# Diagonals in the transposes of the attention, and turned orders at four seams of a two-block kernel

## The reference

```python
h = rms_norm(x, g_mix) * (1 + sc1) + sh1          # sc, sh, gt from silu(c) @ w_ada + b_ada
qa, ka, va, fb, qc, kc, vc = mixer_inputs(h, w_in, ...)   # projection, head norms, rope
o = concat([global_attention(qa, ka, va, ctx...), fourier_mix(fb), window_attention(qc, kc, vc, ctx..., sink)])
x = x + gt1 * (o @ w_out)
x = x + gt2 * swiglu(rms_norm(x, g_ffn) * (1 + sc2) + sh2, w_gate, w_up, w_down)
```

```python
proj = rmsnorm(x, norm_g) @ w_in                   # 8388 columns: three attentions, their gates, merge gates
ya, yb, yc = block-sparse, top-64 and dilated attention, each * silu(its gate)
merged = g0 * (ya @ w_br_a) + g1 * (yb @ w_br_b) + g2 * (yc @ w_br_c)
x = x + merged @ w_out
```

## Time and profile before

| | us |
|---|---|
| median of 3 runs | 1604.14 (1603.93 to 1605.23) |
| profiled execution, device time | 1607.49 |
| its span | 1605.5 |
| PE busy in the span | 1538.0 |
| DVE busy | 935.6 |
| ACT busy | 672.3 |
| POOL busy | 327.1 |

### The profile page before, as it was taken

How to read it: one execution, slowest core, us unless ns; L and a number is a source line. 1 busy time by engine, 2 the same in 40 slices (tenths; PEclk the granted TensorE clock), 3 DMA queues, 4 the chain that set the end, 5 groups by cost and what they waited for, 6 DMA issues and landing times.

```text
span 1605.5 us, 23813 instructions
## 1 busy us (share of the span) xinstructions
PE 1538.0 (96%) x9443; PEld 1268.4 (79%) x9443; DVE 935.6 (58%) x1315; ACT 672.3 (42%) x1051; POOL 327.1 (20%) x267
## 2 busy tenths in 40 slices
PE   5999899999999999999999999899999999999997
PEld 3765458988888888875789998789988878898886
DVE  2745436345434456855466667788634667874356
ACT  3445444311212212535443333654454546455553
POOL 1226521100000000416200000421145211203431
PEclk9999999999999999999999999999999999999999
DMA  8437742233233232338645554645423445462342
GB/s 326 160 105 252 270 109 79 79 105 98 85 105 95 88 106 79 106 125 311 168 133 187 184 184 151 201 154 177 152 86 119 155 152 180 150 189 86 117 138 88
DMA packets 168992, 234.22 MB, mean 146 GB/s; under 512 B 8977, under 2 KB 116537, under 8 KB 168769
## 3 DMA queue, kind: packets, MB, share of 16 engines
q1 hardware_dynamic: 168896, 232.90, 45.0%
HBM read 231.83 MB, written 1.05 MB: 145 GB/s over the span
## 4 chain that ended last, share of the span: by engine, by line
PE 85%; DVE 7%; ACT 3%; DMA 2%; POOL 2%; issue 1%; SPq 0%; POOLq 0%; DVEq 0%; ACTq 0%
PE psum L713 23%; PE psum L715 23%; PE psum L714 23%; PE psum L988 3%; PE psum L1021 3%; PE psum L1008 2%; PE psum L728 2%; DVE wl L1689 2%; DMA raw<-in_w_ada 2%; PE psum L993 1%; ACT wh L1289 1%; PE psum L916 1%; DVE smax L1976 1%; PE psum L848 1%; POOL work L2412 1%
## 5 line engine op out<-in xcount | busy, mean ns | idle before, releaser
L1689 DVE TENSOR_TENSOR wl<-raw,wh 128x2048 fp32r<-128x2048 f32 (+1 forms) x170 | 388.0, 2282 | 255.8 <-ACT wh L1583 150.1
L713 PE MATMUL psum<-hTh,wh 128*128 128x256 f32 (+1 forms) x1376 | 429.0, 312 | 10.4 <-DVE hTl L1797 3.8
L714 PE MATMUL psum<-hTl,wh 128*128 128x256 f32 (+1 forms) x1376 | 424.5, 308 | 0.0
L715 PE MATMUL psum<-hTh,wl 128*128 128x256 f32 (+1 forms) x1376 | 424.3, 308 | 0.0
L713 PEld LDWEIGHTS psum<-hTh,wh 128*128 128x128 f32 x1376 | 263.6, 192 | 27.4 <-issue 7.0
L714 PEld LDWEIGHTS psum<-hTl,wh 128*128 128x128 f32 x1376 | 263.7, 192 | 12.9
L715 PEld LDWEIGHTS psum<-hTh,wl 128*128 128x128 f32 x1376 | 263.8, 192 | 12.5
L1583 ACT ACTIVATE wh<-raw 128x2048 fp32r<-128x2048 f32 x62 | 118.9, 1917 | 364.5 <-PE psum L715 364.5
L1289 ACT ACTIVATE wh<-raw 128x2048 fp32r<-128x2048 f32 (+2 forms) x108 | 202.4, 1874 | 117.2 <-PE psum L715 111.5
L713 PE MATMUL psum<-wh,hTh 128*128 128x512 f32 (+3 forms) x576 | 221.9, 385 | 14.7 <-DVE hTl L1797 6.1
L2412 POOL TENSOR_SCALAR work<-work,share 128x256 f32<-128x256 f32 (+4 forms) x118 | 168.0, 1435 | 297.8 <-DVE share L1992 297.7
(11 more groups left out here) (185 smaller groups left out, 1833.2 us busy)
## 6 DMA issues: line engine op xcount, KB each, us to landing
raw<-in_w_in SPq DMA_DIRECT2D x54, 1024.0 KB, 4.9
raw<-in_w_ada SPq DMA_DIRECT2D x48, 1024.0 KB, 5.9
raw<-in_w_gate SPq DMA_DIRECT2D x22, 1024.0 KB, 5.1
raw<-in_w_up SPq DMA_DIRECT2D x22, 1024.0 KB, 5.2
raw<-in_w_down SPq DMA_DIRECT2D x22, 1024.0 KB, 4.8
raw<-in_w_in SPq DMA_DIRECT2D x16, 768.0 KB, 4.4
raw<-in_w_out SPq DMA_DIRECT2D x8, 1024.0 KB, 4.9
raw<-in_w_out SPq DMA_DIRECT2D x16, 384.0 KB, 7.6
```

The source lines that it names most:

```text
L713: pe.matmul(o, left[0], right[0], start=first, stop=False)
L714: pe.matmul(o, left[0], right[1], start=False, stop=False)
L715: return pe.matmul(o, left[1], right[0], start=False, stop=last)
L1689: dve.tensor_tensor(wl[:, w % SPLIT, 0:m], raw[:, u % RING, 0:m], wh[:, w % SPLIT, 0:m].bitcast(F32), ALU.subtract).then_inc(lo_ready, 1)
```

## The change

There are two kinds of edits. In the attention GpSimd's multiplication is gone. VectorE makes from the shares two diagonal matrices of 128x128 per step (identity times share), and TensorE turns each chunk with an ordinary matmul by its half's diagonal, which turns and scales at once. The lag in att1 goes from 3 to 2. The rest are orders at the seams: wout1 waits at first for all but the last pair and the last Fourier part, and for those before its second half; wout2 goes on with the bank after the merge's last; the output weights of wout1 are loaded only when the last modulation half has been used; in proj2 of layer 0 the residual's normalisation and the masks' rounding stand behind block 1; VectorE's splits at the first step and near the last of an att2 are left for the next one; the gate halves come one slot later.

```diff
-TURN_LAG = (3, 2)
-HALF_GATES = [(1, 1) if i in (7, 8, 9, 10, 11) else (0, 1) if i == 18 else (1, 0) for i in range(19)]
+TURN_LAG = (2, 2)
+HALF_GATES = [(1, 1) if i in (8, 9, 10, 11, 12) else (0, 1) if i == 18 else (1, 0) for i in range(19)]
...
+        shares_first = [scr[:, 3, SEQ * n:SEQ * n + SEQ].rearrange("p (x q) -> p x q", x=2) for n in range(4)]
+        shares_second = [x.rearrange("p (x q) -> p x q", x=2) for x in (
+            csil[:, :, :].rearrange("p k j -> p (k j)"), qkg[:, :, :, :].rearrange("p a l d -> p (a l d)"))]
...
-            return ada_slots(l) + 2 * n_four(l), 2 * (6 * len(tiles_of(l)) + 4) - 3 * l
+            return ada_slots(l) + 2 * n_four(l), 2 * (6 * len(tiles_of(l)) + TURN_LAG[0] + 1) - 3 * l
...
+                if step == "wout1":
+                    behind_ada[len(units)] = plan_count.now(ada_half)
...
+                if u in behind_ada:
+                    sp.wait_ge(ada_half, behind_ada[u])
...
-                    pe.wait_ge(prob_ready, 2 * u["step"] + 2)
+                    pe.wait_ge(share_ready, u["step"] + 1)
+                    diagonal = u["shares"]
...
-                            mm = pe.transpose(o[:, P * x:P * x + P], u["score"][:, f:f + P], ident[:, :])
+                            mm = pe.matmul(o[:, P * x:P * x + P], u["score"][:, f:f + P], diagonal[:, f // u["w"], :],
+                                           start=True, stop=True, skip_group_check=True)
...
-            def wout(tiles, lhs, merged=False, in_last={}):
-                pj[0] = 0
+            def wout(tiles, lhs, merged=False, in_first={}, in_last={}):
+                if not merged:
+                    pj[0] = 0
...
-                    pe.wait_ge(mix_split, pairs_until("att1", l))
-                    pe.wait_ge(mixT_ready, c.now(mixT_ready))
+                    pe.wait_ge(mix_split, pairs_until("att1", l) - 3)
+                    pe.wait_ge(mixT_ready, c.now(mixT_ready) - 1)
+
+                    def last_mixed():
+                        pe.wait_ge(mix_split, pairs_until("att1", l))
+                        pe.wait_ge(mixT_ready, c.now(mixT_ready))
+
...
+                    wout(tiles_of(l), lambda n, t: mixT(n, P * t, P * t + P, False), in_first={(1, 0): last_mixed},
+                         in_last=in_last)
...
+                            if b == 1 and l == 0:
+                                rows_normed()
+                                dve.wait_ge(masks_loaded, 16)
+                                own(dve.tensor_copy(masks2r[:, :, :, :], masks2), masks_rounded)
...
-                    dve.reciprocal(share[:, s, :], total[:, s, :]).then_inc(share_ready, 1)
+                    link(dve.reciprocal(share[:, s, :], total[:, s, :]))
+                    if i >= u["shares_after"]:
+                        dve.wait_ge(turned, steps[i - u["shares_after"]]["turn1"])
+                    dve.tensor_tensor(u["shares"], ident[:, :].unsqueeze(1).broadcast_to([P, 2, P]),
+                                      share[:, s, :].unsqueeze(2).broadcast_to([P, 2, P]), ALU.mult)\
+                        .then_inc(share_ready, 1)
...
+                behind = TURN_LAG[0] + 2
...
-                        split_ahead()
+                        if i not in (0, n + 3):
+                            split_ahead()
...
-            def attention(steps):
-
-                for i, u in enumerate(steps):
-                    pool.wait_ge(share_ready, u["step"] + 1)
-                    for x in range(2):
-                        p = u["score"][:, x * u["w"]:x * u["w"] + u["w"]]
-                        pool.tensor_scalar(p, p, share[:, i % 4, x:x + 1], None, ALU.mult).then_inc(prob_ready, 1)
```

More of the change, by code:

```diff
@@ L344, in build_program @@
         share_ready = sem("share_ready")
-        prob_ready = sem("prob_ready")
         turned = sem("turned")
@@ L479, in build_program @@
                 u["score"] = held[:, 0:2 * u["w"]]
+                kept = shares_first if step == "att1" else shares_second
+                u["shares"], u["shares_after"] = kept[i % len(kept)], len(kept)
                 u["probT"] = work[:, at_t:at_t + 2 * u["w"]].rearrange("p (c q) -> p c q", q=P)
@@ L502, in build_program @@
         ffn_first = {}
+        behind_ada = {}
         def kview(w, k0, k1, c0, c1):
@@ L1086, in wout @@
                     wide((unit[0], unit[0] + 1), [(lambda n, t=t: left(n, t), 0, 512) for t in tiles], 512, evac_dve,
-                         in_front=in_last if hf else {})
+                         in_front=in_last if hf else in_first)
                     unit[0] += 2
@@ L1239, in _ @@
                         in_last = {(1, 3, 2): lambda: turn_rows("norm1b", 0, 0, by_tile=False)}
-                    wout(tiles_of(l), lambda n, t: mixT(n, P * t, P * t + P, False), in_last=in_last)
+                    wout(tiles_of(l), lambda n, t: mixT(n, P * t, P * t + P, False), in_first={(1, 0): last_mixed},
+                         in_last=in_last)
                 if step == "merge2":
@@ L1424, in lead @@
                         act.activation(hi, ps[OUT][:, 0:SEQ], ACT.Copy).then_inc(mix_lead, 1)
-                behind, lag = 4, TURN_LAG[second]
+                lag = TURN_LAG[second]
+                behind = 4 if second else lag + 1
                 for i in range(len(steps) + behind):
@@ L1851, in norm2, with rows_normed @@
                 c.next(rstd_ready, 2)
-                if l:
-                    return
+            def rows_normed():
                 for t in X:
@@ L2016, in attention @@
                         gate(i - 4)
-                    if not second and 0 <= i - 5 < n:
-                        keep_mixed(i - 5)
+                    if not second and 0 <= i - behind < n:
+                        keep_mixed(i - behind)
                     if i < n:
@@ L2073, in wout @@
             def wout(tiles, gated):
-                pj[0] = 0
+                if gated:
+                    pj[0] = 0
                 for hf in range(2):
@@ L2278, in _ @@
                     picks = index_picks()
-                    if l == 0:
-                        dve.wait_ge(masks_loaded, 16)
-                        own(dve.tensor_copy(masks2r[:, :, :, :], masks2), masks_rounded)
                     proj(SECOND_BLOCKS, jobs2, False, l)
@@ L2439, in _ @@
                     proj(SECOND_BLOCKS, jobs2, False)
-                if step in ("att1", "att2"):
-                    attention(att[step, l])
                 if step == "gates2":
```

## The result

The changed kernel takes 1635.36 us (median of four, 1634.74 to 1636.70) against 1604.68 us for the kernel before: a ratio of 1.0194, interval 1.0181 to 1.0208, so +30.7 us. The prediction was 1629.4 us (+25.3), range 1612 to 1643. The profiled execution took 1634.82 us.

What follows compares the result with a forecast made beforehand. The prediction took TensorE to set the time. Turns cost 40.3 us, less 18.5 of waits that go, plus 3.5 that come: +25.3 us on the median of 1604.14, so 1629.4 us, range 1612 to 1643.

Steps and rivals of the forecast that it cites:

- The rival "faster": Attention turns: diagonal matmuls run nearer a transpose's pace, only the waits are left; -15 us, about 1589; chance 0.02.
- The rival of four times: Attention turns: an fp32 matmul costs four times a transpose; 126 us more, 1730 us; chance 0.01.
- the price of a turn: Attention on TensorE: each of 384 transposes made a diagonal matmul costs 0.105 us more, 40.3 us in all.
- Waits that go: TensorE's waits over the whole run that the change removes: together 18.5 us, at most 23.4.
- those that come: New waits at the ends of the first block's attentions, from later output weights: 3.5 us (0 to 10).
- GpSimd, 4.3 taken: Attention: of TensorE's 4.8 us of waits for GpSimd's scaling, 4.3 go.
- The low part of the last mixed pair: Merges and first output projections: of 5.7 us in four waits for this low part, 5.2 go.
- the bank: Second output projection: keeping the bank order avoids a 1.25 us wait, twice; 0.55 gained each, 1.1 us.
- Second projection, 2.5 taken: Layer 0: of TensorE's 3.0 us wait while VectorE normalises and rounds before splitting weights, 2.5 go.
- Modulation weights and gates: First-attention modulation transfers, clock included: 4.5 of 5.5 us go; waits on gate read-outs: 0.9 of 1.9 us go.
- The late output weights: First-block attention ends: output weights go out some 8 us later, ScalarE stands some 5 us; 3.5 us taken.
- rival 2: Ends of both first attentions: ScalarE blocks for the output weights' landing, about 5 us more each; +35 to +45; chance 0.12.

Runs made afterwards that it cites:

- experiment 2: Changed kernel with plain transposes against the identity; diagonals still made and waited for, division by the sums left out: 1599.58 us.
- experiment 6: Changed kernel without the hold on the output weights, VectorE scaling probabilities in place instead of making diagonals, turns by transposes, lag 2: 1592.31 us.
- experiment 8: Changed kernel without the hold on the output weights, with probabilities and diagonals written in the rounded format: 1593.83 us.
- experiment 3: Kernel before with the attention part alone: diagonals on VectorE, matmuls with them, lag 2; orders, gate slots and loads as before: 1643.46 us.
- experiment 1: Changed kernel without the sync queue's wait that holds the first block's output weights until the last modulation half is used: 1629.55 us.
- experiment 10: Experiment 9 with the second output projection starting again with the first PSUM bank, as in the kernel before: 1594.26 us.
- experiment 5: Changed kernel with the attention of before (GpSimd scales, transposes, lag 3) and without the hold on the output weights: 1593.04 us.
- experiment 9: Experiment 6 with lag 3 in place of 2 in the first block's attention: 1590.15 us.

## Why the prediction was right in sign and 6 us short

**The mechanism holds.** TensorE sets the time; a transpose became an fp32 product of two records; nothing hides it. Experiments 2, 6 and 8, which change this and little else, give 35.7 to 37.2 us back, more than the whole loss of 30.7. The rival "faster" (the diagonal form near a transpose's pace) is shown wrong for this form, and right for the rounded one. The rival of four times is wrong: the Trainium skill's page TensorE: Matmul & The Clock Gate (section Terms) calls the transpose mode four times faster for FP32, and here the spacing is 0.117 us more on a turn of about 0.124, a factor of 1.95.

**The term that was mis-sized: the price of a turn.** "I take 0.105 us, between the two" was too low; the trace has 0.117, above the upper bound of 0.114. The 0.223 us came from a group of 32 records, in which one change-over is spread over 16 products; a group of turns has 16 records and pays one for every 8 chunks, 1.930 / 8 = 0.241 us. The right comparison was group against group: 16 records of 0.112 us and a change-over, against 8 of 0.109 and a change-over, 0.99 us before and some 1.9 after. It is 45 us gross instead of 40.3.

**Waits that go, less those that come: the trace has 14.4 us of idle time less, the prediction 15.0** (18.5 less 3.5). Its parts:
- GpSimd, 4.3 taken. The 4.8 us are gone, but the diagonals come late in their place: 3.4 us of waits in experiments 3 and 1, 1.9 us in the changed kernel. So 1.4 to 2.9 us were gained. The prediction put VectorE's new work at 0.
- The low part of the last mixed pair and the bank, 5.2 + 1.1 = 6.3 taken. By start times the gaps ahead of the first output projections shrink by 1.8 and 1.1 us, and the two merges with what follows by 2.0 each: 6.9. The bank's part, 1.1 taken, is 1.3 by experiment 10.
- Second projection, 2.5 taken: TensorE's wait for the low weights there is 1.0 us instead of 3.0. Over the whole run these waits fall only from 4.1 to 3.7 us; smaller ones came elsewhere, 0.8 us of them behind the first merge.
- Modulation weights and gates, 4.5 + 0.9 taken: the waits for the transfers fall from 11.3 to 6.9 us over the run, by 4.4, and the 1.9 us of waits for a gate's read-out are gone altogether. The reason given for the first was in part wrong: holding back the output weights has no share in it (experiments 1 and 3).
- The late output weights, 3.5 taken. The hold is 8.0 us long in layer 0, as predicted. Here rival 2 half came true: its mechanism is there in both layers, ScalarE standing for 6.20 and 6.09 us, at about half its size. Experiments 1 and 5 price it at 5.8 and 5.3 us by their medians, 4.6 and 3.8 within the attentions. What was missing is the clock: the stalls of TensorE are 3.7 and 2.0 us, and 5 us at 0.67 follow each.

So the stages of the first block were forecast too short (+6 to 12 and +7 to 11; measured +15.6 and +14.5), because both mis-sized terms lie there. The second block's (+3 to 7 each) came out at 3.9 and 4.0.

**What was added to what.** Between the profiled executions the difference is 1634.82 - 1607.49 = 27.3 us, 2 us more than the sum of 25.3. The other 3.4 us of the miss are the base: the profiled execution of before ran 2.8 us over the median of its four runs. A part of it can be seen. Windows of 20 us of the kernel before, at the norms behind the first block and at the second projection, and of the changed kernel at the same work:

```profile
802.00:822.00 20.00, 16.29 (x112) 14.96 (x111) 11.93 (x17) 12.68 (x21) 3.50 (x6) 0.91 0.30 95
...
1018.00:1038.00 20.00, 16.99 (x78) 14.73 (x77) 16.29 (x23) 8.72 (x11) 6.90 (x5) 0.91 0.49 152
```

```profile
829.00:849.00 20.00, 15.49 (x117) 14.26 (x116) 12.52 (x16) 12.68 (x21) 3.38 (x6) 1.00 0.29 93
...
1045.00:1065.00 20.00, 19.00 (x100) 16.67 (x99) 14.56 (x22) 12.41 (x15) 3.45 (x4) 1.00 0.58 178
```

Where TensorE idles for some 4 us in the first of them, the clock dipped in the one profile and not in the other. The second dip is another matter. It came right behind the 3.0 us wait that the change shortens; timeline of the kernel before:

```profile
1022.53 0.47 PE L713 MATMUL psum<-wh,hTh 128*128 128x452 f32 x1 [3.01 <-DVE wl L1689]
```

So it may be a gain of the orders that the prediction did not count. Over the whole spans the mean granted clock was 0.993 before and 0.995 after. As an estimate, 0.007 x 1605.5 = 11.2 us and 0.005 x 1633.0 = 8.2 us went to the lower clock, 3 us less, and 41.9 + 3 is the 45 us of the turns. The sum should have been put on the profiled time, as the prediction also did (1632.8 against 1634.82), or the dips taken out first.

**Where the other 9 us of experiment 2 are.** The changed kernel and experiment 2 differ by 35.8 us, while the gross price is 45. In the profiled executions 5.2 us are waits that shorter turns uncover (idle time 53.1 and 58.3 us). Most of the rest is the clock: 0.995 over 1633.0 us against 0.992 over 1597.8 us, by the estimate above 8.2 and 12.8 us. 45 - 5.2 - 4.6 = 35.2 us, the difference of the two spans.

**Left open.** That the change is some 3 us better than the sum of its halves was not taken apart. Of the orders only the bank and the hold of the output weights were tested by themselves; the shares of the others are read from start times and waits.

## What to carry to other kernels

Where TensorE is the bound, count its records: moving a scaling from an idle engine into a transpose can pay only if the turn stays one record, and a VectorE with room does the same scaling in place at no cost that these runs can tell (1592.31 and 1590.15 us, against 1593.04 with GpSimd). Price a replaced instruction by the start of its group to the start of the next, for groups of the size that it will have, not by a busy mean or by a longer group. When a load is held back for one reader, look up what stands first in the queue of the engine that waits for it: here that engine also reads out TensorE's results, and the hold cost 4 to 6 of the 12 us that the other orders gave.

## What the runs showed of the hardware

- An fp32 product of 128x128 by 128 columns is two records, 0.112 us apart. On rounded operands it is one, and as fast as a transpose: groups of eight take 0.985 and 0.990 us (medians).
- The same stretch with the same idle time is granted different clocks. In experiments 9 and 10, at the norms behind the first block (windows of 9, then of 10):

```profile
798.00:818.00 20.00, 15.66 (x95) 14.24 (x94) 12.32 (x16) 10.92 (x22) 3.62 (x7) 0.83 0.28 87
...
998.00:1018.00 20.00, 16.50 (x67) 13.03 (x66) 13.47 (x17) 12.08 (x27) 10.77 (x14) 0.83 0.61 199
```

```profile
798.00:818.00 20.00, 15.48 (x114) 14.14 (x113) 12.49 (x17) 13.11 (x23) 3.67 (x7) 1.00 0.27 89
996.00:1016.00 20.00, 15.88 (x77) 12.73 (x76) 14.73 (x19) 12.10 (x28) 13.00 (x15) 1.00 0.64 205
```

From the end of the second attention to the start of the third experiment 9's profiled execution takes 3.4 us longer than experiment 10's, though nothing in their code differs there. That is more than one of this change's orders is worth, so a single profile can't judge such an edit. What decides whether the clock falls was not found.
- The executions of one kernel differ with the mean granted clock. Experiment 2's seven run from 1596.42 us at 0.995 to 1603.12 us at 0.988, experiment 5's five from 1590.97 us at 0.998 to 1597.96 us at 0.992. Two medians of such kernels should be compared at like clocks.
- Short stalls can suffice: behind waits of 3.7, 2.0 and 1.7 us the clock was 0.67, 0.67 and 0.65 for some 5 us, which costs about 1.7 us each time on top of the wait.
